# Expert rows added by the DMA to the residual rows in memory, in place of a buffer of two rows per token

## The reference, cut to what matters

```
h = h + hybrid_mixer(rms_norm(h, mix_norm_w), ...)
xn = rms_norm(h, ffn_norm_w)
for each token: two experts e1 != e2 with weights w1, w2
y[token] = w1 * ffn(e1, xn[token]) + w2 * ffn(e2, xn[token])
ffn(e, x) = (silu(x @ w_gate[e]) * (x @ w_up[e])) @ w_down[e]
h = h + y
out = rms_norm(h, final_norm_w)[16:]        # the 16 meta tokens are dropped
```

## Time and profile before

| | us |
|---|---|
| median of 3 runs | 1504.84 |
| lowest, highest | 1503.98, 1507.54 |
| the profiled execution | 1506.76 |
| its span, first to last instruction | 1504.9 |

### The profile page before, as it was taken

How to read it: one execution, slowest core, us unless ns; L and a number is a source line. 1 busy time by engine, 2 the same in 40 slices (tenths; PEclk the granted TensorE clock), 3 DMA queues, 4 the chain that set the end, 5 groups by cost and what they waited for, 6 DMA issues and landing times.

```text
span 1504.9 us, 20632 instructions
## 1 busy us (share of the span) xinstructions
PE 1318.8 (88%) x7574; PEld 1144.4 (76%) x7574; DVE 932.9 (62%) x1178; ACT 722.3 (48%) x927; POOL 158.7 (11%) x145
## 2 busy tenths in 40 slices
PE   3989998999899989769993389999999999999960
PEld 3979997999799989547772278888888888888840
DVE  4664455445544554332225578888888888888827
ACT  6351234134313430232222067777777777777823
POOL 0010111011102110011110011111111111111000
PEclk9999998999899999659996599999999999999985
DMA  6100010000000000243330379999999999999848
GB/s 194 43 15 29 15 43 16 29 29 29 16 29 29 29 15 26 87 149 103 93 99 23 137 279 356 370 378 383 382 389 372 382 382 379 375 376 377 328 176 334
DMA packets 37141, 274.39 MB, mean 182 GB/s; under 512 B 8053, under 2 KB 8309, under 8 KB 23773
## 3 DMA queue, kind: packets, MB, share of 16 engines
q1 hardware_dynamic: 27032, 250.88, 45.3%
q0 software_dynamic: 9216, 17.06, 3.0%
q10 hardware_dynamic: 837, 5.63, 1.1%
HBM read 260.57 MB, written 29.49 MB: 193 GB/s over the span
## 4 chain that ended last, share of the span: by engine, by line
PE 64%; DVE 13%; ACT 10%; issue 10%; DMA 2%; DVEq 0%; SPq 0%; ACTq 0%; POOLq 0%; POOL 0%
PE bank L1127 7%; PE bank L1129 7%; PE bank L1128 7%; PE bank L511 6%; PE bank L513 6%; PE bank L512 6%; DVE w_lo L744 5%; ACT w_hi L623 4%; PE bank L1245 4%; PE bank L1243 3%; PE bank L435 3%; PE bank L436 3%; PE bank L437 3%; ACT xgT_hi L641 2%; DVE arena L897 1%
## 5 line engine op out<-in xcount | busy, mean ns | idle before, releaser
L744 DVE TENSOR_TENSOR w_lo<-w_raw,w_hi 128x2048 fp32r<-128x2048 f32 x192 | 433.3, 2285 | 68.9 <-ACT w_hi L623 68.9
L623 ACT ACTIVATE w_hi<-w_raw 128x2048 fp32r<-128x2048 f32 x192 | 357.3, 1917 | 17.4 <-PE bank L513 14.3
L1127 PE MATMUL bank<-xn_hi,p_hi 128*128 128x346 f32 (+1 forms) x672 | 229.9, 342 | 0.0
L1129 PE MATMUL bank<-xn_hi,p_lo 128*128 128x346 f32 (+1 forms) x672 | 217.1, 323 | 0.0
L1128 PE MATMUL bank<-xn_lo,p_hi 128*128 128x346 f32 (+1 forms) x672 | 217.0, 323 | 0.0
L511 PE MATMUL bank<-w_hi,xgT_hi 128*128 128x512 f32 x512 | 206.7, 404 | 2.9 <-DVE xgT_lo L890 2.9
L513 PE MATMUL bank<-w_hi,xgT_lo 128*128 128x512 f32 x512 | 201.0, 393 | 0.0
L512 PE MATMUL bank<-w_lo,xgT_hi 128*128 128x512 f32 x512 | 200.7, 392 | 0.0
L1127 PEld LDWEIGHTS bank<-xn_hi,p_hi 128*128 128x128 f32 x672 | 128.6, 191 | 0.4
L1128 PEld LDWEIGHTS bank<-xn_lo,p_hi 128*128 128x128 f32 x672 | 128.2, 191 | 0.3
L1129 PEld LDWEIGHTS bank<-xn_hi,p_lo 128*128 128x128 f32 x672 | 127.6, 190 | 0.0
(11 more groups left out here) (237 smaller groups left out, 2072.9 us busy)
## 6 DMA issues: line engine op xcount, KB each, us to landing
w_raw<-in_w_down SPq DMA_DIRECT2D x32, 2048.0 KB, 9.9
w_raw<-in_w_gate SPq DMA_DIRECT2D x31, 2048.0 KB, 10.6
w_raw<-in_w_up SPq DMA_DIRECT2D x31, 2048.0 KB
p_raw<-in_w_tiles SPq DMA_DIRECT2D x28, 512.0 KB, 3.5
arena<-in_tokens SPq DMA_DIRECT2D x20, 416.0 KB
arena<-y_rows SPq DMA_DIRECT2D x8, 1024.0 KB, 11.9
h_rows<-arena SPq DMA_DIRECT2D x10, 416.0 KB
xn_rows<-arena SPq DMA_DIRECT2D x10, 416.0 KB
```

What stands on the lines that cost most here:

```text
L623: nc.scalar.activation(w_hi[m][:, half], wraw[m][:, half], ACT.Copy).then_inc(hi_done[m], 1)
L744: nc.vector.tensor_tensor(w_lo[m][:, half], wraw[m][:, half], w_hi[m][:, half].bitcast(F32), ALU.subtract).then_inc(lo_done[m], 1)
L1127: nc.tensor.matmul(out[:, 0:n], p_hi[slot][:, k, :], hi, start=(k == 0), stop=False)
L1129: m = nc.tensor.matmul(out[:, 0:n], p_lo[slot][:, k, :], hi, start=False, stop=(k == KD - 1))
```

## The change: what it does

- `y_rows` is gone. The scatter of a block goes to the token's row in `h_rows`, and the DMA adds to what is there (`compute_op=ALU.add`). The table `dst` holds the token number for both choices.
- Two blocks may now hold the same token, so their scatters must not overlap: each scatter from the second on waits until the one before it, which came from the other buffer, has landed.
- POOL also waits for `h_stored` before its first gather.
- The last stage loads the 8 tiles of `h_rows` alone, all after `moe_done`. The 8 loads of `y_rows` (8.4 MB) and DVE's 16 additions are gone. ACT starts on a tile when its load has landed.
- ACT's Exp waits for DVE's multiply two tiles earlier, since that one reads the same place of `stat`.

```diff
-    put("dst", (2 * tok[:, :, None] + np.arange(2)[None, None, :] - BIG).reshape(C, 2 * NC))
+    put("dst", np.repeat(tok - BIG, 2, axis=1))
...
-        y_dram = nc.dram_tensor("y_rows", (2 * L, D), F32, kind="Internal").ap()
...
-        yf = [zf.take(2 * D) for _ in range(FT)]
...
             total = sp.value_load(over_i[0:1, OVER:OVER + 1], min_val=0, max_val=OVER)
+            sp.wait_ge(moe_done, 1)
             for t in range(FT):
                 if t % 4 == 0:
                     sp.wait_ge(lo_done[t // 4], (total + E) * 2)
                 sp.dma_start(hf[t], h_dram[META + t * 128:META + (t + 1) * 128, :]).then_inc(hf_loaded[t], 16)
-
-            sp.wait_ge(moe_done, 1)
-            y_v = y_dram.rearrange("(t k) d -> t (k d)", k=2)
-
-            for t in range(FT):
-                sp.dma_start(yf[t], y_v[META + t * 128:META + (t + 1) * 128, :]).then_inc(yf_loaded[t], 16)
...
                 u = t % 2
-                act.wait_ge(f_add, t + 1)
+                act.wait_ge(hf_loaded[t], 16)
...
                 act.wait_ge(f_stat, 2 * t + 2)
+                if t >= 2:
+                    act.wait_ge(f_out, t - 1)
                 nc.scalar.activation(stat[:, u, 2:3], stat[:, u, 1:2], ACT.Exp, scale=-0.5).then_inc(f_rstd, 1)
...
-            for t in range(FT + 1):
-                if t < FT:
-                    dve.wait_ge(hf_loaded[t], 16)
-                    dve.wait_ge(yf_loaded[t], 16)
-                    nc.vector.tensor_tensor(hf[t], hf[t], yf[t][:, 0:D], ALU.add).then_inc(f_sum, 1)
-                    dve.wait_ge(f_sum, t + 1)
-                    nc.vector.tensor_tensor(hf[t], hf[t], yf[t][:, D:2 * D], ALU.add).then_inc(f_add, 1)
-                if t:
-                    rstd = stat[:, (t - 1) % 2, 2:3]
-                    dve.wait_ge(f_rstd, t)
-                    nc.vector.scalar_tensor_tensor(of[t - 1], hf[t - 1], rstd, fw, ALU.mult, ALU.mult).then_inc(f_out, 1)
+            for t in range(FT):
+                dve.wait_ge(f_rstd, t + 1)
+                nc.vector.scalar_tensor_tensor(of[t], hf[t], stat[:, t % 2, 2:3], fw, ALU.mult, ALU.mult).then_inc(f_out, 1)
...
-                nc.gpsimd.indirect_dma_start(out=y_dram, out_offset=bass.IndirectOffsetOnAxis(ap=si[p], axis=0),
-                                             in_=ysb[p], in_offset=None,
-                                             bounds_check=last_choice, oob_is_err=False).then_inc(scattered[p], 16)
+                if e and e < E:
+                    pool.wait_ge(scattered[1 - p], (e + 1) // 2 * 16)
+                nc.gpsimd.indirect_dma_start(out=h_dram, out_offset=bass.IndirectOffsetOnAxis(ap=si[p], axis=0),
+                                             in_=ysb[p], in_offset=None, bounds_check=last_row, oob_is_err=False,
+                                             compute_op=ALU.add).then_inc(scattered[p], 16)
...
             pool.wait_ge(x2_stored, 16 * NC)
+            pool.wait_ge(h_stored, 16 * NC)
```

More of the change, by code:

```diff
@@ L336, in layer_kernel @@
         fw_loaded = sem("fw_loaded")
-        f_sum, f_add, f_stat, f_rstd, f_out = sem("f_sum"), sem("f_add"), sem("f_stat"), sem("f_rstd"), sem("f_out")
+        f_stat, f_rstd, f_out = sem("f_stat"), sem("f_rstd"), sem("f_out")
         f_stored = sem("f_stored")
         FT = (L - META) // 128
-        hf_loaded, yf_loaded = [[sem(f"{n}_loaded{t}") for t in range(FT)] for n in ("hf", "yf")]
+        hf_loaded = [sem(f"hf_loaded{t}") for t in range(FT)]
         hf = [wraw[t // 4][:, t % 4 * D:(t % 4 + 1) * D] for t in range(FT)]
         zf = Zone(GBASE + 2 * WU, NF)
-        yf = [zf.take(2 * D) for _ in range(FT)]
         of = [zf.take(D) for _ in range(FT)]
@@ L950, in tail_vector @@
             dve.wait_ge(fw_loaded, 16)
-            for t in range(FT + 1):
-                if t < FT:
-                    dve.wait_ge(hf_loaded[t], 16)
-                    dve.wait_ge(yf_loaded[t], 16)
-                    nc.vector.tensor_tensor(hf[t], hf[t], yf[t][:, 0:D], ALU.add).then_inc(f_sum, 1)
-                    dve.wait_ge(f_sum, t + 1)
-                    nc.vector.tensor_tensor(hf[t], hf[t], yf[t][:, D:2 * D], ALU.add).then_inc(f_add, 1)
-                if t:
-                    rstd = stat[:, (t - 1) % 2, 2:3]
-                    dve.wait_ge(f_rstd, t)
-                    nc.vector.scalar_tensor_tensor(of[t - 1], hf[t - 1], rstd, fw, ALU.mult, ALU.mult).then_inc(f_out, 1)
+            for t in range(FT):
+                dve.wait_ge(f_rstd, t + 1)
+                nc.vector.scalar_tensor_tensor(of[t], hf[t], stat[:, t % 2, 2:3], fw, ALU.mult, ALU.mult).then_inc(f_out, 1)
         def tail_pool(pool):
-            last_row, last_choice = pool.to_reg(L - 1), pool.to_reg(2 * L - 1)
+            last_row = pool.to_reg(L - 1)
             pool.wait_ge(oy_done, H)
```

## The result

The change made the kernel slower: 1513.1 us median (1509.47 to 1516.77, 11 runs) against 1506.3 us (1503.98 to 1509.86, 11 runs) before, ratio 1.0044 with a 95% interval of 1.0031 to 1.0057. That is 0.4%, small but clear of the noise. The forecast was 1493 us and faster.

A forecast was written before the change was run, and what follows sets the result against it. PE was taken to pace the expert stage at 18.12 us a block, with DMA nearly full. Last stage -13.9 plus expert stage +2.0 gave -11.9 us: median 1504.84 to 1493, own range 1489 to 1498, 8-in-10 range 1489 to 1516.

The forecast's parts named there:

- The last stage: End of the kernel: loading h alone, without DVE's 16 additions, ends the span at 1491.0 instead of 1504.9, 13.9 us saved.
- the two sums: Last stage: ACT's tile chain ends at 1490.7 us, the DMA's 8.39 MB at 426 GB/s at 1490.5; 1491.0 taken.
- The last scatter: Start of the last stage: the adding scatter also reads, so lands 1.0 us later, within bounds of 0 to 2.8.
- The price of an added row: Expert-stage scatters: an added row takes double a copied row's DMA time, adding 0.275 MB a block.
- the ceiling: Expert stage: DMA rising from 376 to 391 GB/s stays nearly free, since one block ran at 406; 2 us allowed.
- the DMA is already full, and every added microsecond shows: Rival, expert stage: 98.2% share becomes 102.1%, costing some 11 us over 29 blocks; 1502 us, chance 0.18.
- The stall rival: Expert-stage DMA: engines wait for each old row, costing 52 us over 29 blocks; 1543 us, anything from 1508; chance 0.25.
- The new waits: Scatter for the previous scatter, Exp for the multiply two tiles back, and `h_stored`: all forecast to cost nothing.
- The moved loads of h: Last stage: four early loads of h, formerly hidden beside the last block's products, are now on the path and counted.

The follow-up runs named there:

- loads by halves: Each weight matrix loaded in two halves, each half reissued once split: on the kernel after 1508.55 us, ratio 1.0012; on the kernel before 1509.0 us, ratio 1.0013.
- the lightened before: The kernel before with only half of each down matrix loaded except the first, 1 MB a block left out: 1507.24 us, ratio 1.0005.
- the lightened after: The kernel after with the same 1 MB of down-matrix weights a block left out, adds kept: 1494.6 us, ratio 0.9916 to the kernel before.

## Why the prediction was wrong, point by point

**The last stage** was right in kind and its time was forecast 1.7 us too short. Forecast: first load to the span's end 22.65 us (1468.35 to 1491.0); measured 24.35, against 37.55 before. ACT started 3.67 us after the issue (3.6 forecast) and then took 1.60 us a tile, better than the 1.8. The last multiply ended 17.9 us after the first load, 19.35 forecast. But from there to the end it was 6.5 us, not 3.05: the stores stood behind the loads. Of the two sums, the DMA's decided. Its mis-sized term was the rate, as this window shows (columns as in the earlier trace rows):

```profile
1485.20:1509.00 23.80, 0.00 (x0) 0.00 (x0) 10.26 (x8) 12.40 (x32) 0.00 (x0) 0.50 0.91 353
```

8.39 MB after a start of 2.4 us took 21.95, which is 382 GB/s and not 426. The forecast had the rate "held at 426 GB/s for tiles of other sizes", and no row shows that. It was read while tiles of y moved, whose packets are 8 KB, and the packets of h and of the output are 4 KB. The packet records give 309 ns for one of 8 KB (before, 1469.30 to 1487.30) and 159 for one of 4 KB (after, 1499 to 1508); 16 engines at these paces make 424 and 412 GB/s, an estimate. The tiles of h alone, before the first store at 1491.95, moved 397 and 404 GB/s at shares of 1.00 and 1.02 (1487.20 to 1489.20, 1489.20 to 1491.90). Between loads and stores there is a gap besides, 315 GB/s at a share of 0.89 from 1495 to 1499.

**The last scatter**: 1.0 us more was taken, 2.7 measured, at the upper bound of the range given (2.8).

**The price of an added row** was right: twice a copied one. The queue shares of the kernel after and its packets (327 ns against 159) show it, and the kernel with two copies a row has the same shares. The Trainium skill's rule of two source reads ("Collectives: The Full Stack", section "The bandwidth ceiling: the fold count and why AG ≠ RS ≠ AR") agrees with these traces: 11.5% with adds, 11.4% with two copies.

**The step that failed is the ceiling**: "The block from 1094.67 ran at 406 and was not longer", so that 391 GB/s would be free. It was not. One block at 406 is no proof of a rate that can be held; why that block showed 406 was not looked into. The five blocks at 387 had a share of 1.00, so they had nothing left either. 426 was read from the last stage, from a long run of 8 KB packets without gaps, and says nothing of a stage with three loads and two lists of rows a block. What the stage could hold was close to what it was already moving: 376 GB/s before, 377 with two copies, 379 with adds, 381 with adds and loads by halves (the uncounted old rows put in). For the expert stage the sum allowed 2 us, and 16.2 were measured. By the Trainium skill's "Perfetto Trace Analysis", section "Roofline", some 435 GB/s are a core's bound. The longest stretch of loads here ran at 426, and the expert stage's own limit lay 11 to 12% below that.

**The rival that came true** is "the DMA is already full, and every added microsecond shows", at 0.18. Its reading of the share, 98.2% with q0's half doubled, was the right one; it gave 11 us, and the stage lost 16.2. Its sum for the trace, 2.9 us shorter, was still 7.5 off the 4.6 longer that was measured: 5.2 in the stage, 1.7 at the last scatter and 1.7 in the last stage, less 1.3 before the first gather. The argument held against it, that an open packet is not a working engine because the share was 0.99 at 368 GB/s and 1.01 at 406, was wrong where it mattered: with 1 MB less a block the share falls to 90.4% and the loss is gone. There is something in it all the same: the lightened before moved 15% fewer bytes than before, and its share fell by 11% only (98.2 to 87.2%). A share of 98% means full here, but a share is not in proportion to the bytes. The blocks now last 18.8 us at a share of 97.6%, about 0.4 us of it gaps; the loads by halves closed some and won back 4 us. That fits the part over the 11.

**The stall rival** fell: its price would have been 52 us in the expert stage. 1513.1 lies in the times it was given (1508 on) and within the range of 1489 to 1516, but only by luck: slower was to come from rows that cost four copies or more, and they cost two. **The new waits** cost nothing, as forecast (ratio 0.9999). **The moved loads of h** were rightly put on the path.

Two things stay open. Why the stage holds 376 to 381 GB/s where loads alone held 426 was not tried. The packet records of the kernel before narrow it down: a 16 KB packet of weights takes 611 ns in the median (16 engines at that pace would make 429 GB/s, an estimate) but 684 on the average, since one in ten takes 820 or more; what holds these up is not shown. And why the loss is 16 and not 11 was argued from shares; the loads by halves account for 4 us of it.

## What to carry to other kernels

A transfer that disappears from one stage may have to be paid for in another: here 8.4 MB of reads and 16 additions left the last stage, which gave 13 us, and some 8 MB of reads of old rows, which the profile does not count, came into a stage whose DMA share was already 98%, where they cost 16. For room in the DMA read the sum of the queues' shares over many blocks, not the highest rate of a single window, and count an adding scatter as two copies. Put work where the share is low: the same add for the last two blocks alone, with the y loads beside the last block's products, made the kernel before 0.5% faster.

## What the runs showed of the hardware that was not expected

- The profile's MB do not count the row that an adding scatter reads: 15.01 MB and 11.5% of the engines for adds, 22.22 MB and 11.4% for two copies. An adding packet of 4 KB takes 327 ns, a plain one 159.
- POOL's instruction for an adding scatter is longer, 2.00 us on the average against 1.00, and in a full stage that of the gathers behind it too; with room in the DMA the gathers are short again. From the groups of POOL's instructions (busy us, mean ns), the kernel after and the lightened after:

```profile
L972 POOL DMA_INDIRECT arena<-xn_rows,arena x32 | 65.2, 2038 | 85.5 <-DVE arena L880 53.9 <-DVE arena L876 12.4 <-DVE arena L900 10.4
L981 POOL DMA_INDIRECT h_rows<-arena x32 | 64.1, 2004 | 466.2 <-ACT arena L649 466.2
```

```profile
L984 POOL DMA_INDIRECT h_rows<-arena x32 | 50.7, 1585 | 490.9 <-ACT arena L652 490.9
L975 POOL DMA_INDIRECT arena<-xn_rows,arena x32 | 37.1, 1159 | 85.6 <-DVE arena L883 53.9 <-DVE arena L879 12.3 <-DVE arena L903 10.6
```

- An adding scatter that is alone in the DMA lands after 5.1 to 5.5 us, a plain one of the same rows after 2.8.
- DVE's additions and multiplies of 128 x 1024 float32 take 3.35 us in place of 1.21 while POOL adds tiles of the same shape. POOL's additions take 2.33 us at the least and 3.32 in the median. The Trainium skill says in "SBUF — State Buffer", section "SBUF: two separate sides", that a DVE instruction with two inputs in SBUF and a GpSimd instruction that reads SBUF need the same pair of ports; whichever starts first holds it for the whole instruction, and the other is blocked. This trace fits: both sit at 3.3 us, which is the 1.21 of one and some 2.1 of the other in turn.
